# Where weights stream and where the input streams: the two operands' places modulo 64 bytes, swapped by stage

## The reference, cut to what matters

```
qkv = xn @ w_qkv                      # attention mixers: 1024 -> 3072
c   = xn @ w_in                       # low-rank mixer: 1024 -> 672
g   = xn @ w_gate; u = xn @ w_up      # feed-forward: 1024 -> 2816 twice
h   = act(conv3(g) + conv_b) * u
out = h @ w_down                      # 2816 -> 1024
```

## Time and profile before

| | before |
|---|---|
| median of the runs | 1073.62 us |
| the profiled execution's own time | 1073.9 us |
| its span | 1072.1 us |
| TensorE busy | 1066.1 us |
| VectorE busy | 838.6 us |
| ScalarE busy | 655.9 us |
| granted TensorE clock, whole span | full speed (2.4 GHz) |

### The profile page before, as it was taken

One profiled execution on the slowest core, in us unless ns is written; L12 is line 12 of the kernel. 1 busy time (PEld: TensorE's weight loads), 2 busy tenths in 40 slices (PEclk: granted clock), 3 DMA queues, 4 the chain that ended last, 5 costly groups with the idle time before them and its releaser, 6 DMA issues.

```text
span 1072.1 us, 16292 instructions
## 1 busy us (share of the span) xinstructions
PE 1066.1 (99%) x6536; PEld 932.2 (87%) x6536; DVE 838.6 (78%) x1364; ACT 655.9 (61%) x922; POOL 1.3 (0%) x8
## 2 busy tenths in 40 slices
PE   9999999999999999999999999999999999999998
PEld 7778988888898888888889888888877788888888
DVE  7985799876668779987767999876668768997852
ACT  6666567655367766766456577654456765776540
POOL 0000000000000000000000000000000000000000
PEclk9999999999999999999999999999999999999999
DMA  8543446555426145655552366555555433665540
GB/s 312 202 179 119 140 175 236 196 186 216 148 89 261 44 184 180 223 215 177 215 196 92 138 221 232 186 216 187 184 180 182 149 124 145 236 217 194 202 144 30
DMA packets 32092, 191.67 MB, mean 179 GB/s; under 512 B 4497, under 2 KB 6161, under 8 KB 12177
## 3 DMA queue, kind: packets, MB, share of 16 engines
q1 hardware_dynamic: 32016, 190.62, 50.2%
HBM read 189.56 MB, written 1.05 MB: 178 GB/s over the span
## 4 chain that ended last, share of the span: by engine, by line
PE 94%; DVE 3%; ACT 1%; DMA 1%; issue 1%; SPq 0%; DVEq 0%; ACTq 0%
PE banks L463 21%; PE SB L463 11%; PE TB L463 11%; PE banks L465 11%; PE TB L465 6%; PE SB L465 6%; PE banks L679 4%; PE banks L686 4%; PE banks L680 4%; PE banks L422 3%; PE banks L424 3%; PE banks L423 3%; PE banks L636 2%; PE TB L610 2%; PE SB L597 1%; DMA raw<-in_a_first 1%
## 5 line engine op out<-in xcount | busy, mean ns | idle before, releaser
L1712 DVE TENSOR_TENSOR wlo<-raw,whi 128x2048 fp32r<-128x2048 f32 (+2 forms) x180 | 395.8, 2201 | 75.9 <-ACT whi L1173 75.8
L1173 ACT ACTIVATE whi<-raw 128x2048 fp32r<-128x2048 f32 (+2 forms) x180 | 330.5, 1840 | 81.4 <-PE TB L465 25.6
L463 PE MATMUL banks<-xx,whi 128*128 128x512 f32 x752 | 262.2, 390 | 0.2 <-DVE wlo L1712 0.2
L465 PE MATMUL banks<-xx,wlo 128*128 128x256 f32 x752 | 212.1, 282 | 0.0
L463 PEld LDWEIGHTS banks<-xx,whi 128*128 128x128 f32 x752 | 141.1, 188 | 30.1 <-DVE wlo L1712 0.5
L465 PEld LDWEIGHTS banks<-xx,wlo 128*128 128x128 f32 x752 | 142.1, 189 | 0.0
L463 PE MATMUL TB<-xx,whi 128*128 128x512 f32 x336 | 117.8, 390 | 0.2 <-DVE xx L1717 0.2
L463 PE MATMUL SB<-xx,whi 128*128 128x512 f32 x320 | 111.8, 390 | 0.0
L465 PE MATMUL TB<-xx,wlo 128*128 128x256 f32 x336 | 94.7, 282 | 0.0
L463 PE MATMUL banks<-hx,whi 128*128 128x512 f32 x264 | 91.7, 390 | 0.0
L465 PE MATMUL SB<-xx,wlo 128*128 128x256 f32 x320 | 90.2, 282 | 0.0
(11 more groups left out here) (244 smaller groups left out, 1943.4 us busy)
## 6 DMA issues: line engine op xcount, KB each, us to landing
raw<-in_gate SPq DMA_DIRECT2D x44, 1024.0 KB, 4.8
raw<-in_up SPq DMA_DIRECT2D x44, 1024.0 KB, 4.8
raw<-in_down SPq DMA_DIRECT2D x32, 1024.0 KB, 4.8
raw<-in_down SPq DMA_DIRECT2D x16, 768.0 KB, 4.1
raw<-in_d_kq SPq DMA_DIRECT2D x8, 1024.0 KB, 5.0
raw<-in_a_kq SPq DMA_DIRECT2D x6, 1024.0 KB, 5.3
raw<-in_a_o SPq DMA_DIRECT2D x4, 1024.0 KB, 4.9
raw<-in_b_o SPq DMA_DIRECT2D x4, 1024.0 KB, 5.3
```

Source lines behind the costliest of these rows:

```text
L463: e.matmul(po[:, 0:512], wh[:, k, sl], a[:, kk, :, :].rearrange("p w s -> p (w s)"), start=start, stop=stop, skip_group_check=True)
L465: return e.matmul(po[:, 0:256], wl[:, k, sl], a[:, kk, 0, :], start=False, stop=stop, skip_group_check=True)
L1173: e.activation(whi[n % RING][:, 0:nk * w], raw[n % RAW][:, 0:nk * w], ACT.Copy).then_inc(s_hi, 1)
L1712: e.tensor_tensor(wlo[n % RING][:, 0:nk * w], raw[n % RAW][:, 0:nk * w], whi[n % RING][:, 0:nk * w].bitcast(F32), ALU.subtract).then_inc(s ...
```

## The change

The change gives each operand its place by the stage that uses it. The ring tensors `whi` and `wlo` get 64 bytes more, `xx` 32 bytes more. A new function `parts` returns a unit's floats either from the start of the ring tensor or from 8 floats (32 bytes) further on: the latter for the units of A and DD that hold query, key and value weights (`a_kq`, `a_v`, `d_kq`, `d_v`), for `b_inkv`, `b_inq` and for `pool`. A new function `x_of(s)` returns the block's input 32 bytes further on in stages A, B, DD and POOL, and at the start of `xx` in F0 to F3. All writers (L1173, L1176, L1665, L1712, L1717, L2304) and all matmuls go through these two. A second pad of 32 bytes stands ahead of `con`.

After it the places are these. In the first products of the mixers weights move at place 32 and `xx` is stationary at place 0. In the feed-forward parts nothing changes modulo 64. `raw`, `gx`, `con`, `hx`, `ox` and all else keep their places modulo 64. Modulo 128 some move: ring tensor number i of `whi` starts 64 i bytes later than before and number i of `wlo` 64 (5 + i) bytes later, all tensors from `con` on 704 bytes later.

```diff
-        whi = [sb(f"whi{i}", [128, UNIT], F32R) for i in range(RING)]
-        wlo = [sb(f"wlo{i}", [128, UNIT], F32R) for i in range(RING)]
+        whi = [sb(f"whi{i}", [128, UNIT + 16], F32R) for i in range(RING)]
+        wlo = [sb(f"wlo{i}", [128, UNIT + 16], F32R) for i in range(RING)]
...
-        xx = sb("xx", [128, KD, 2, S], F32R)
+        xx = sb("xx", [128, 8 + KD * 2 * S], F32R)
+        off_line("constants")
...
+        def parts(n):
+
+
+            name, _, nk, w = plan[n]
+            at = 8 if name[:3] in ("a_k", "a_v", "d_k", "d_v") or name in ("b_inkv", "b_inq", "pool") else 0
+            return whi[n % RING][:, at:at + nk * w], wlo[n % RING][:, at:at + nk * w]
+
         def unit(n):
...
+            return tuple(x.rearrange("p (k n) -> p k n", k=plan[n][2]) for x in parts(n))
+
+        def x_of(s):
+
+            at = 8 if s in MIX or s == POOL else 0
+            return xx[:, at:at + KD * 2 * S].rearrange("p (k w s) -> p k w s", k=KD, w=2)
...
-                    last = across_wide(u, bg, k, xx, k, k == 0, k == KD - 1)
+                    last = across_wide(u, bg, k, x_of(s), k, k == 0, k == KD - 1)
...
-                    e.matmul(po, xx[:, k, 0, sl], wh[:, k % 4, :], start=k == 0, stop=False, skip_group_check=True)
+                    e.matmul(po, x_of(s)[:, k, 0, sl], wh[:, k % 4, :], start=k == 0, stop=False, skip_group_check=True)
...
-                e.activation(whi[n % RING][:, 0:nk * w], raw[n % RAW][:, 0:nk * w], ACT.Copy).then_inc(s_hi, 1)
+                e.activation(parts(n)[0], raw[n % RAW][:, 0:nk * w], ACT.Copy).then_inc(s_hi, 1)
```

More of the change, by code:

```diff
@@ L557, in ffn @@
                     for k in range(KD):
-                        last = across_wide(n, bg, k, xx, k, k == 0, k == KD - 1)
+                        last = across_wide(n, bg, k, x_of(s), k, k == 0, k == KD - 1)
                         if s == F2 and i == 1 and k == 0:
@@ L567, in ffn @@
                     for k in range(KD):
-                        last = across_wide(n + 1, bu, k, xx, k, k == 0, k == KD - 1)
+                        last = across_wide(n + 1, bu, k, x_of(s), k, k == 0, k == KD - 1)
                     last.then_inc(s_used, 1)
@@ L678, in high @@
                     po = slot_bank(s, i, h)[:, :]
-                    e.matmul(po, xx[:, k, 0, sl], wh[:, k % 4, :], start=k == 0, stop=False, skip_group_check=True)
-                    e.matmul(po, xx[:, k, 1, sl], wh[:, k % 4, :], start=False, stop=False, skip_group_check=True)
+                    e.matmul(po, x_of(s)[:, k, 0, sl], wh[:, k % 4, :], start=k == 0, stop=False, skip_group_check=True)
+                    e.matmul(po, x_of(s)[:, k, 1, sl], wh[:, k % 4, :], start=False, stop=False, skip_group_check=True)
                 def low(i, h, k):
@@ L685, in low @@
                     sl = slice(h * 128, (h + 1) * 128)
-                    return e.matmul(slot_bank(s, i, h)[:, :], xx[:, k, 0, sl], wl[:, k % 4, :], start=False,
+                    return e.matmul(slot_bank(s, i, h)[:, :], x_of(s)[:, k, 0, sl], wl[:, k % 4, :], start=False,
                                     stop=k == KD - 1, skip_group_check=True)
@@ L899, in latent_half @@
                             x_here(s, kk)
-                        last = three(b[:, 0:w], xx[:, kk, 0, sl], xx[:, kk, 1, sl], wh[:, k, :], wl[:, k, :],
+                        last = three(b[:, 0:w], x_of(s)[:, kk, 0, sl], x_of(s)[:, kk, 1, sl], wh[:, k, :], wl[:, k, :],
                                      kk == 0, kk == KD - 1)
@@ L1122, in linear @@
                             sl = slice(h * 128, (h + 1) * 128)
-                            last = three(b[:, h * 256:(h + 1) * 256], xx[:, k, 0, sl], xx[:, k, 1, sl], wh[:, k, :],
+                            last = three(b[:, h * 256:(h + 1) * 256], x_of(s)[:, k, 0, sl], x_of(s)[:, k, 1, sl], wh[:, k, :],
                                          wl[:, k, :], k == 2 * g and h == 0, k == 2 * g + 1)
@@ L1664, in hi_quarter @@
                 e.wait_ge(s_first[n][q], 16)
-                last = e.activation(whi[n][:, at], raw[n][:, at], ACT.Copy)
+                last = e.activation(parts(n)[0][:, at], raw[n][:, at], ACT.Copy)
                 last.then_inc(s_hi if q == 3 else s_hq, 1)
@@ L1711, in lo @@
                 e.wait_ge(s_hi, n + 1)
-                e.tensor_tensor(wlo[n % RING][:, 0:nk * w], raw[n % RAW][:, 0:nk * w],
-                                whi[n % RING][:, 0:nk * w].bitcast(F32), ALU.subtract).then_inc(s_lo, 1)
+                e.tensor_tensor(parts(n)[1], raw[n % RAW][:, 0:nk * w], parts(n)[0].bitcast(F32), ALU.subtract).then_inc(s_lo, 1)
             def split_x(s, k):
                 e.wait_ge(s_xh, n_x(s, k))
-                e.scalar_tensor_tensor(out=xx[:, k, 1, :], in0=xT[:, k, :], scalar=gain_of(s, k),
-                                       in1=xx[:, k, 0, :].bitcast(F32), op0=ALU.mult,
+                e.scalar_tensor_tensor(out=x_of(s)[:, k, 1, :], in0=xT[:, k, :], scalar=gain_of(s, k),
+                                       in1=x_of(s)[:, k, 0, :].bitcast(F32), op0=ALU.mult,
                                        op1=ALU.subtract).then_inc(s_xl, 1)
@@ L2303, in lo_quarter @@
                     e.wait_ge(s_hi, n + 1)
-                e.tensor_tensor(wlo[n][:, at], raw[n][:, at], whi[n][:, at].bitcast(F32),
+                e.tensor_tensor(parts(n)[1][:, at], raw[n][:, at], parts(n)[0][:, at].bitcast(F32),
                                 ALU.subtract).then_inc(s_lo if q == 3 else s_lq, 1)
```

16 lines of the change are left out of this document (4 added, 12 removed).

## The result

The change made the kernel slower. The changed kernel takes 1081.08 us (median of four runs, 1080.84 to 1081.29), the kernel before, beside it on the same chip, 1073.69 us. The ratio is 1.0068, with a 95% interval of 1.0056 to 1.008, so some 7.4 us. I had forecast 1071.8 us in a range of 1070.5 to 1074.1.

The account below looks back on a forecast made before the run. The prediction took the kernel as a nearly unbroken row of TensorE matmuls. Savings of 1.67 us (first products) and 0.10 (B), about 1.8, from the median 1073.62 gave 1071.8 us, range 1070.5 to 1074.1.

Parts of the forecast that it names:

- Feed-forward parts and all else: F0 to F3 and the rest: nothing moves modulo 64, so 0; moves modulo 128 were left to a slow rival.
- a rival at 0.11: Slower, 1078.8 us: stationary weights starting 64 bytes off a multiple of 128 cost 2120 matmuls 3.2 ns each, 6.8 us; chance 0.11.
- The place to look: If A's distances fell but the time did not: F0, where a pair mean above 0.3467 us, split by unit, shows the price.
- The first products of A and DD: L679, L680, L686: 522 of 576 matmuls save 3.2 ns each, 1.67 us; ends 0 and 2.40 us.
- no effect: Rival: A's extra cycles belong to the width and the row's rhythm, not to places; 1073.6 us; chance 0.23.
- The straight line 8 + 17/16 N: Cycles for N columns at the feed-forward places, from F0's pairs and 256-column steps; gives 552 cycles, 0.2300 us, for 512.
- my lower end of 228.5: Lowest price for 512 columns: F0's pair less POOL's 256 columns, 0.3467 - 0.1182 = 0.2285 us; saves 4.6 ns a matmul.
- the larger gain: Rival: 512 columns take 0.2285 us, saving 2.40 + 0.17 = 2.6 us, for 1071.0 us; chance 0.17.
- B and POOL: `b_inkv` saves 0.07 us and `b_inq` 0.03; POOL's 0.07 stands ahead of a wait and counts nothing; ends 0 and 0.17.
- The writers: ScalarE and VectorE copies to the new places, 17 units and some 32 chunks: hidden, 0; uncovered, a microsecond or less.

Follow-up runs that it names:

- e1: Kernel before with ring tensors 64 bytes longer, nothing 32 bytes further on, a pad keeping `xx` and all after it in place; 1079.42 us, ratio 1.0054.
- e2: Changed kernel with ring tensors 256 instead of 64 bytes longer and a pad keeping `xx`, `con`, `hx`, `ox` at old places; 1073.96 us, ratio 1.0002.
- e4: Map on the kernel before, ring tensors 256 bytes longer: each unit's weights shifted 0 to 224 bytes by 32s; gate and up pairs 345.5 to 353.7 ns.
- e5: Against e2, the block's input stays at the start of `xx`; only the mixers' first-product weights lie 32 bytes further on; 1071.72 us, ratio 0.998.
- e8: Second map like e4, feed-forward shifts in 16-byte steps up to 112, other shifts in A and DD; one gate unit of F1 at 340.0 ns a pair.
- e7: Kernel before with one 96-byte pad ahead of `whi0`, so all operands move together and keep their distances; 1073.77 us, ratio 0.9999.
- e12: Kernel before with ring tensors 256 bytes longer, weights at the tensor's start, the block's input 224 bytes further on in mixers and POOL; 1071.58 us, ratio 0.998.
- e9: Against e5, feed-forward and output-projection high weights 96 bytes and low weights 48 bytes further on; 1071.59 us, ratio 0.9978 to the kernel before.
- e11: As e9, but gate unit 1 of each feed-forward part has high weights at 80, low at 48 bytes; 1061.21 us, ratio 0.9876 to the kernel before.

## Why the prediction was wrong

*The step that failed* is "Feed-forward parts and all else. Modulo 64 nothing moves, so 0." It measured +7.06 us. The 64 bytes that make room for the shift give each ring number another distance to `xx` and `hx` modulo 256 (e1 has such a loss without the swap, e2 has the swap without the loss). I had seen that places modulo 128 move and priced it as a rival at 0.11; its 6.8 us are near the measured 7.06, but by a mechanism that e1 and e4 refute. By it each ring place would have paid 3.2 ns for one of its two halves, while in the gate and up units place 1 pays nothing and places 0 and 4 pay 6.4 to 6.6 ns. The size is a coincidence. The place to look was named rightly: pairs of F0, split by unit.

*The first products of A and DD* were to fall from 233.1 to 230.0 ns, for 1.67 us. In the changed kernel they take 232.8 ns, and freed of the stride (e2) 233.3. The step compared two kinds of code in which moving and stationary places, and with them the distance, differed together, and read a rule for places out of it. The change moves both operands by the same 32 bytes, so apart from the stride their distance stays. Had I asked what is invariant, "no effect" would have been the forecast for this part. The straight line 8 + 17/16 N came from two widths and isn't a floor: at distance 0 the 512 columns take 228 ns (e5). That this is near my lower end of 228.5 is chance, since I got that end from a difference of two prices at other places. I had also read 48 extra cycles in 512 columns as far above 24 in 256, where the two are in proportion; it gave the larger gain a reason that it did not have.

*B and POOL* were too small to matter: in the changed kernel 288 columns take 132.5 ns, 384 take 175.1 and POOL's 256 take 117.7, against 130.8, 173.3 and 116.7 forecast. In e2 they take 132.3, 173.8 and 118.2, as before the change; there the swap does nothing either.

*The writers* cost nothing, as said: the VectorE and ScalarE sums differ by 0.3 and 0.1 us. The units that write to the new place are 29 and not 17 (12 each in A and DD, four in B, one in POOL); nothing hung on it.

*Rules that I had weighed.* The Trainium skill, "SBUF — State Buffer", section "Door 1: The DMA port swizzle", has lines of 16 bytes, with a penalty for each access that crosses to a new line. It says nothing of starts that differ by whole lines, and e8's 233.3 ns at a shift of 16 bytes against 227 to 228 at 32 shows that these can differ in price. The Trainium skill, "TensorE: Matmul & The Clock Gate", section "Wait — 56ns, not 53.3ns?", gives 215.7 ns for 512 columns; no unit's mean here is below 226. The same page of the Trainium skill, section "Part 2: What happens when you issue a matmul", has two independent read ports, so that loading the next weights takes no read bandwidth from the running matmul. No row here shows a port. What the runs show is that a common move of both operands costs nothing (e7), and that with another distance 512 columns go from 233 to 228 ns (e2 against e5 and e12), so how the two lie to each other does have a price.

*What stays open.* Why a distance is good or bad is not shown; a clash of the weight load's reads with the moving rows' reads is what D suggests, and no row shows a read. The distances 32 and 96 cost 350.0 or 346.7 ns, and nothing here says which when. The entry into the 340 ns rhythm was copied from one unit, not derived; in e9 the end of DD led into it without that unit. No kernel was run with a stride that is a multiple of 128 and not of 256.

## What to carry to other kernels

Where weight loads run beside matmuls in float32r, keep the strides of ring buffers a multiple of 256 bytes, as 8192 and 8448 were here and 8256 was not, so that a pad for one purpose doesn't give every ring place another distance between the operands. To tune such a row of matmuls, change the distance between stationary and moving operand (here 0 modulo 256 for 512 columns of moving weights gave 5 ns a matmul) instead of the place of either, and let one run map many distances, one for each unit. Read the result as start-to-start time by unit: a mean over the kernel hides that units fall into different rhythms, and a rhythm once entered can hold for hundreds of matmuls. Here it was lost where one load came 50 ns late, so the step at which it ends is worth finding.

## What the hardware showed that I had not expected

The same pairs of 512 and 256 columns ran at 340.0, 344.4, 346.7, 349 to 350 and 353.3 ns, at the full granted clock and with no wait; at 2.4 GHz 340.0, 346.67 and 353.33 ns are 816, 832 and 848 cycles, steps of 16. At equal distances a stage ran at 346.7 or 340.0 ns according to one unit of 16 pairs run first (e9, e11), and the 340 ns rhythm ended at two matmuls of another kind (e9) and at one late weight load (e11). The same program's executions split into times 3.1 us apart (e11), about what the rest of F2 costs in the slower rhythm.
